# Stick-breaking attention: the weighted sums of two spans in one run of TensorE, every second step

## The chip, the cores and the metric

The kernel runs on one core of a Trainium2 chip. The metric is the device time of one execution in microseconds (us), from the profile of that core or from timed runs without a profile.

## What is computed

One step of a two-layer decoder: a retention layer, a projection to shared keys and values, and a layer of stick-breaking attention over them. The change lies in the attention of that last layer, for a prompt of 1024 tokens, 16 heads of width 64, and for eight sample sequences of 8 new tokens over 256 cached ones:

```python
z = jnp.einsum('bqhd,bkhd->bhqk', qi, k).astype(F32) * scale + bias_f
mask = (k_pos[None, :] < pi[:, None])[None, None]
log_keep = jnp.where(mask, jax.nn.log_sigmoid(-z), 0.0)
tail = lax.cumsum(log_keep, axis=3, reverse=True)
tail_excl = jnp.concatenate([tail[..., 1:], jnp.zeros_like(tail[..., :1])], axis=-1)
w = jnp.where(mask, jnp.exp(jax.nn.log_sigmoid(z) + tail_excl), 0.0)
return jnp.einsum('bhqk,bkhd->bqhd', w, v)
```

The kernel takes the products of the keeps, sigmoid(-z), instead of sums of their logarithms: `keep` is sigmoid(-z), `take` is sigmoid(z), and a weight is `take` times the running product of the keeps of all later keys.

## The kernel before

The attention is cut into pieces (`pieces`, lines 1389 to 1403). Heads go in eight pairs; a pair has eight blocks of 128 queries (a unit, 64 in all); a unit is taken in one or two spans of at most 512 keys; a span of over 256 keys makes two pieces, one for each head, and a narrower one makes one piece with both heads. A piece "closes" when the weights of both heads of its span exist: the piece of head 1, or the only one. With the eight sample pieces in the second half there are 168 pieces, numbered from 0; 96 of the prompt's pieces close.

Every engine walks through the pieces in program order, one step for each piece. At step p:

- TensorE (PE) runs `score(p + 1)` (L1768, L1769: two products for each head into one of two banks `z`), then in some steps `turn_pages` (L1744, cached keys of a sample), then `turn_w(p - 3)` (L1778: 128x128 transposes of the finished weights into one of two banks `wt`), then `attend(p - 4)`, which does nothing for a piece that does not close, and for one that does multiplies the turned weights of both heads with the values (L1806: matmuls of 64 columns, two side by side in the array, 2 for each 128 keys). In between, in the first half, `project` puts slices of three matmuls (L2959 to L2961) of the projection of the gates, in three places of a step. `fold` and `attend_sample` (L1836, L1827) belong to the samples.
- ScalarE (ACT) runs `stick(p)` (L1917: `keep`, then `take`), then `take_w(p - 3)` (L1928: copies the turned weights from `wt` to the ring `w_t`) for two pieces of three, and opens gates now and then (L1962).
- VectorE (DVE) runs `scan(p - 1)` (L2029), `take_w(p - 3)` (L2038) for every third piece, and `gate` (L2085), the product of a finished block of sums with the gates.
- GpSimd (POOL) runs `weigh(p)` (L1705), `take` times the scanned products.

Two waits tie PE to ACT. `score(p + 1)` waits until `stick(p - 1)` has emptied its bank `z`. ACT reaches `stick(p - 1)` only after `take_w(p - 5)`, the copy of a piece that PE turned in step p - 2. `attend(p - 4)` waits for the copy of piece p - 4, and it does so for pieces that do not close too:

```python
            def attend(p):
                at = pieces[p]
                wait_taken(pe, p)
```

The ring `w_t` has WR = 4 slots: a copy of piece p waits until the sums that read piece p - 4 are done. The gates' projection ends at step 65 (`G_END`); after it SP loads the inputs of the samples (`load_samples`), and at step 71 PE turns the first of them (`turn_new`, L1731). SP loads the values of a pair (`load_v`) 4 steps after the pair before it has ended. A row of biases is loaded to `bias_row` (L2624) and copied by DVE to `bias` (L2822), long before the attention starts. After the last piece PE goes on with the first products of the output layer (L1889).

Of the kernel before, what the change touches and what calls it, by code (L numbers as in the profile page):

```python
# [23 lines left out]
P = 128  # L24
# [3 lines left out]
NPT = SEQ // P  # L28
# [9 lines left out]
AH = 16  # L38
# [1263 lines left out]
class PairBuffers:  # L1302


    def __init__(self, nc):
        self.at = at = -(-nc.sbuf_base // 32) * 32

        def sb(name, shape, dt=F32):
            nonlocal at
            made = nc.alloc_sbuf_tensor_at(f"pa_{name}", shape, dt, offset=at)  # L1310
            at += -(-4 * math.prod(shape[1:]) // 32) * 32
            return made

        self.parts = nc.alloc_sbuf_tensor_at("kq_parts_q", [P, 2, 2, NB // P, P], F32R, offset=at)
        self.k_t = sb("k_t0", [P, 2, SEQ], F32R)
        self.q_hi = sb("q_hi0", [P, 2, SEQ], F32R)
        self.gates_at = at
        self.g_t = sb("g_t", [P, 2, SEQ])
        self.head_rows = sb("head_rows", [AH, P])
        self.bias_row = sb("bias_row", [P, AH])  # L1320
        self.bias = sb("bias", [P, 2, AH])
        self.queries_at = at
        self.q_lo = sb("q_lo0", [P, 2, SEQ], F32R)
        self.g_out = sb("g_out", [P, 2, NB])
        self.end = at
# [48 lines left out]
def attention(nc, t_in, t_out, ps, proj, first, sa, held, pairs, kq_stored, ctx, sem):  # L1374


    with ctx:
# [67 lines left out]

        LAG, TR, WR, KR = 3, 5, 4, 3
        sb("pairs", [P, (pairs.end - pairs.at) // 4])
# [121 lines left out]
        def wait_taken(engine, p):  # L1569
# [3 lines left out]
            else:  # L1573
                engine.wait_ge(w_taken_a, len([n for n in range(p + 1) if not on_vector(n)]))

        def sample_before(p, lag):

            return pieces[p - lag].b if p >= lag else None
# [9 lines left out]
        def _(sp):  # L1588
# [50 lines left out]
            load_g(1)  # L1639
            v_slots = {ends[NPT * pair - 1] + 4: pair + 1 for pair in range(1, PAIRS - 1)}  # L1640
            g_slots = {ends[NPT * pair - 1] + 8: pair + 1 for pair in range(1, PAIRS - 1)}
# [81 lines left out]
        def _(pe):  # L1723
# [59 lines left out]
# [3 lines that stand above are left out]
                if at.b is not None:  # L1786
                    attend_sample(p, at.b)
                    return
                if not at.closes:
                    return  # L1790
                if len(at.heads) == 1:
# [68 lines left out]
            for p in range(NPC):  # L1860
# [9 lines left out]
                project(slices_before(p, 1), slices_before(p, 2))  # L1870
                if p >= LAG + 1:
                    attend(p - LAG - 1)
                project(slices_before(p, 2), slices_before(p + 1, 0))
                if p == G_END + 2:
                    turn_gates()
                if sample_before(p, LAG + 3) is not None:
                    fold(sample_before(p, LAG + 3))
            for p in range(NPC, NPC + LAG):
                turn_w(p - LAG)
                attend(p - LAG - 1)  # L1880
            attend(NPC - 1)
            pe.wait_ge(next_loaded, 16)
# [114 lines left out]
        def _(dve):  # L1997
# [91 lines left out]

            def gate_at(p):  # L2090
                if pieces[p].u is not None and p == ends[pieces[p].u] and pieces[p].u % 4 == 3:
                    gate(pieces[p].u)

# [21 lines left out]
            for p in range(NPC):  # L2115
                if p:
                    scan(p - 1)
                if p >= LAG:
                    take_w(p - LAG)
                if p >= LAG + 2:  # L2120
                    gate_at(p - LAG - 2)
                for t in steps_done_at(p):
# [10 lines left out]
            for p in range(NPC - LAG, NPC):  # L2133
                take_w(p)
            for p in range(NPC - LAG - 2, NPC):
                gate_at(p)
# [312 lines left out]
def shared_kv_and_queries(nc, t_in, t_out, ps, x, rated, proj, pairs, kq_stored, handed, block, sem):  # L2449
# [6 lines left out]
    with ctx:  # L2456
# [132 lines left out]
        def _(sp):  # L2589
# [32 lines left out]
            for n in range(2):  # L2622
                sp.wait_ge(parts_stored[n], 16 * NPT // 2)
            sp.dma_start(pairs.bias_row[:], t_in["sb_bias"].to_broadcast([P, AH])).then_inc(consts, 16)  # L2624
            for n in range(2):
# [121 lines left out]
        def _(dve):  # L2747
# [7 lines left out]
            for s, (c, t) in enumerate(steps):  # L2755
# [64 lines left out]
                if c == GATES and t == AHEAD_AT:  # L2820
                    dve.wait_ge(consts, 16)
                    nc.vector.tensor_copy(pairs.bias[:, 0], pairs.bias_row[:])  # L2822
                    nc.vector.tensor_scalar(pairs.bias[:, 1], pairs.bias_row[:], -1.0, None, ALU.mult)

# [399 lines left out]
```

## Time and profile before

| | us |
|---|---|
| median of three timed runs | 1826.2 (1821.4 to 1829.25) |
| the profiled execution | 1827.52 |
| its span in the trace | 1825.9 |
| attention, step 1 to the last copy of weights, about | 1374 to 1715 |
| PE busy over the span | 1773.8 (97%) |
| DVE, ACT, POOL busy | 966.6, 777.1, 266.8 |

Busy time is the union of an engine's instructions. A matmul is pipelined: it is shown for longer than the engine is kept by it, and the next one starts while it is shown. What PE needs for a group of matmuls is therefore read from start to start, not from the durations.

### The profile page before, as it was taken

To read this page: it belongs to the slowest core of one execution; us is meant where nothing else is said; L and a number is where in the kernel's file an instruction comes from. 1 tells how busy PE (TensorE), PEld (TensorE's weight loads), DVE (VectorE), ACT (ScalarE), POOL (GpSimd) and SP (SyncE) were. 2 spreads that over 40 slices of the span, in tenths; PEclk is the share of its full clock that TensorE was granted. 3 is DMA by queue.
4 is the path that set the end of the run, shared out by engine and by line. 5 is a ranking of instruction groups with operands and counts; after the bars stand their busy time and mean duration, and the time that the engine had idled before them with its cause. 6 is when DMAs were issued, how large, how long until landed. Compare 5 with 4: busy or idle time off the path is not lost. (4 is left out here: it accounts for less than half of the span.)

```text
span 1825.9 us, 27331 instructions
## 1 busy us (share of the span) xinstructions
PE 1773.8 (97%) x9783; PEld 1394.7 (76%) x9783; DVE 966.6 (53%) x1836; ACT 777.1 (43%) x1651; POOL 266.8 (15%) x324
## 2 busy tenths in 40 slices
PE   5999999999999999999999999999999999999998
PEld 2778787878787878777787877888877777677677
DVE  4563535353535353543546455676615666877652
ACT  3842323232323232332234333353326677888620
POOL 2000000000000000000000012101114554555300
PEclk8999999999999999999999999999999998999999
DMA  9231313131313131465524578424355557795342
GB/s 335 87 96 60 96 59 95 59 95 59 95 59 95 59 95 59 159 219 153 149 75 137 186 213 271 138 85 130 122 146 129 129 128 237 194 240 179 97 158 98
DMA packets 153688, 240.59 MB, mean 132 GB/s; under 512 B 13208, under 2 KB 102096, under 8 KB 152561
## 3 DMA queue, kind: packets, MB, share of 16 engines
q1 hardware_dynamic: 136570, 179.69, 33.3%
q0 software_dynamic: 17024, 59.66, 9.2%
q8 instruction: 57, 0.93, 0.2%
q14 instruction: 37, 0.30, 0.1%
HBM read 177.91 MB, written 61.42 MB: 131 GB/s over the span
## 5 line engine op out<-in xcount | busy, mean ns | idle before, releaser
L484 PE MATMUL rt_acc<-rt_w_hi,rt_h_hi 128*128 128x512 f32 x504 | 203.3, 403 | 1.0 <-DVE rt_h_lo L1026 1.0
L486 PE MATMUL rt_acc<-rt_w_hi,rt_h_lo 128*128 128x512 f32 x504 | 197.1, 391 | 0.0
L485 PE MATMUL rt_acc<-rt_w_lo,rt_h_hi 128*128 128x512 f32 x504 | 196.5, 390 | 0.0
L1705 POOL TENSOR_TENSOR pa_take<-pa_take,pa_after_key 128x512 f32<-128x512 f32 (+2 forms) x152 | 152.9, 1009 | 140.0 <-DVE pa_after_key L2029 135.1
L1069 DVE TENSOR_TENSOR rt_by_cos<-rt_raw,rt_cos 128x256 f32<-128x256 f32 (+1 forms) x72 | 30.6, 425 | 242.9 <-ACT rt_raw L899 242.9
L910 ACT COPY rt_qk_t<-rt_tr 128x256 f32<-128x256 f32 (+1 forms) x72 | 26.1, 362 | 277.5 <-PE rt_tr L718 277.5
L2971 PE MATMUL kq_acc<-kq_w_hi,kq_h 128*128 128x512 f32 x320 | 128.6, 402 | 0.0
L2974 PE MATMUL kq_acc<-kq_w_hi,kq_h 128*128 128x512 f32 x320 | 125.1, 391 | 0.0
L2972 PE MATMUL kq_acc<-kq_w_lo,kq_h 128*128 128x512 f32 x320 | 124.8, 390 | 0.0
L1917 ACT ACTIVATE pa_keep<-z,pa_bias 128x128 f32<-128x128 f32 (+3 forms) x192 | 111.2, 601 | 2.9 <-PE z L1769 2.5
L1917 ACT ACTIVATE pa_take<-z,pa_bias 128x128 f32<-128x128 f32 (+3 forms) x192 | 111.3, 604 | 0.0
L486 PEld LDWEIGHTS rt_acc<-rt_w_hi,rt_h_lo 128*128 128x128 f32 x504 | 94.6, 188 | 20.6
L484 PEld LDWEIGHTS rt_acc<-rt_w_hi,rt_h_hi 128*128 128x128 f32 x504 | 94.9, 188 | 19.2 <-DVE rt_h_lo L1026 1.4
L485 PEld LDWEIGHTS rt_acc<-rt_w_lo,rt_h_hi 128*128 128x128 f32 x504 | 94.9, 188 | 17.9 <-issue 0.2
L776 PE MATMUL rt_acc_g<-rt_h_hi,rt_g_hi 128*128 128x512 f32 x256 | 105.6, 413 | 0.0
L2029 DVE TENSOR_TENSOR_SCAN pa_after_key<-pa_keep,pa_eye 128x384 f32<-128x384 f32 (+3 forms) x112 | 93.2, 850 | 18.0 <-POOL pa_take L1705 10.5
L777 PE MATMUL rt_acc_g<-rt_h_hi,rt_g_lo 128*128 128x512 f32 x256 | 100.1, 391 | 0.0
L778 PE MATMUL rt_acc_g<-rt_h_lo,rt_g_hi 128*128 128x512 f32 x256 | 100.1, 391 | 0.0
L1778 PE MATMUL pa_wt<-ident,pa_take 128*128 128x128 f32 x592 | 94.7, 278 | 0.8 <-POOL pa_take L1705 0.6
L1778 PEld LDWEIGHTS pa_wt<-ident,pa_take 128*128 128x128 f32 x592 | 71.7, 142 | 19.5 <-POOL pa_take L1705 4.1
L1806 PE MATMUL pa_out<-pa_w_t,pa_v 128*64 128x128 f32 x1152 | 85.3, 284 | 0.9 <-ACT pa_w_t L1928 0.3
L2029 DVE TENSOR_TENSOR_SCAN pa_after_key<-pa_keep,pa_after_key,pa_eye 128x512 f32<-128x512 f32 x64 | 81.7, 1277 | 8.2 <-ACT pa_keep L1917 5.2
(407 smaller groups left out, 4035.8 us busy)
## 6 DMA issues: line engine op xcount, KB each, us to landing
ro_a_raw<-retained SPq DMA_DIRECT2D x14, 1024.0 KB, 5.9
rt_w_raw<-in_ret_w_in SPq DMA_DIRECT2D x16, 512.0 KB, 5.2
rt_w_raw<-in_ret_w_in SPq DMA_DIRECT2D x8, 1024.0 KB, 8.0
rt_old<-in_state_ret SPq DMA_DIRECT2D x8, 1024.0 KB, 6.0
rt_g_raw<-in_ret_w_in SPq DMA_DIRECT2D x8, 1024.0 KB, 5.3
out_st_sample<-rt_new POOLq DMA_DIRECT2D x8, 1024.0 KB, 8.1
k_cols<-kq_parts POOLq DMA_DIRECT2D x16, 512.0 KB, 4.0
kq_w_raw<-in_sb_w_in SPq DMA_DIRECT2D x4, 2048.0 KB, 10.5
```

The lines of the kernel that those rows point to most:

```text
L484: nc.tensor.matmul(dst, h_hi[:, k, cols], w_hi[:, k, :], start=k == 0, stop=False)
L485: nc.tensor.matmul(dst, h_hi[:, k, cols], w_lo[:, k, :], start=False, stop=False)
L486: last = nc.tensor.matmul(dst, h_lo[:, k, cols], w_hi[:, k, :], start=False, stop=k == KD - 1)
L776: nc.tensor.matmul(dst, g_hi[:, k, part], h_hi[:, k, cols], start=k == 0, stop=False)
L777: nc.tensor.matmul(dst, g_lo[:, k, part], h_hi[:, k, cols], start=False, stop=False)
L1705: nc.gpsimd.tensor_tensor(own, own, later, ALU.mult).then_inc(weighed, 1)
L1778: last = nc.tensor.transpose(dst[:, b * P:(b + 1) * P], take(p)[:, b * P:(b + 1) * P], ps.ident[:])
L1917: last = nc.scalar.activation(dst[:, cols], z[:, p % 2, cols], ACT.Sigmoid, scale=(2 * part - 1) * DH ** -0.5, bias=shift)
L2029: nc.vector.tensor_tensor_scan(ring[:, c0:c0 + n][:, ::-1], k[:, ::-1], opening, seed, ALU.mult, join).then_inc(scanned, 1)
L2971: nc.tensor.matmul(dst, hi, w_hi, start=k == 0, stop=False)
L2972: last = nc.tensor.matmul(dst, hi, w_lo, start=False, stop=t == NPT and k == KD - 1)
L2974: last = nc.tensor.matmul(dst, proj.lo(t)[:, k, :], w_hi, start=False, stop=k == KD - 1)
```

## The change

`bias_row` goes, and the row of biases is loaded to `bias[:, 0]`, where it is used. `WR`, the number of slots of the ring of turned weights, goes from 4 to 5. `attend` is no longer called one step after `turn_w` of its piece: closing pieces are held back in twos, and both are summed one after the other four steps behind the second of them. A piece is summed alone where the unit is the last of four of a block of output, or a sample comes. Pieces that do not close are no longer waited for. The gates follow the new order, and SP takes up `load_v` one step later.

```diff
-        self.bias_row = sb("bias_row", [P, AH])
...
-        LAG, TR, WR, KR = 3, 5, 4, 3
+        LAG, TR, WR, KR = 3, 5, 5, 3
...
+        batches, held_back = {}, []
+        for p, at in enumerate(pieces):
+            if at.b is not None and held_back:
+                batches[held_back[-1] + LAG + 1] = held_back
+                held_back = []
+            if at.closes:
+                held_back = held_back + [p]
+            if at.b is not None or len(held_back) == 2 or at.closes and at.last and at.u % 4 == 3:
+                batches[p + LAG + 1] = held_back
+                held_back = []
+        attend_step = {p: step for step, batch in batches.items() for p in batch}
+        gate_step = {attend_step[ends[u]] + 1: u for u in range(3, UNITS, 4)}
...
-            v_slots = {ends[NPT * pair - 1] + 4: pair + 1 for pair in range(1, PAIRS - 1)}
+            v_slots = {ends[NPT * pair - 1] + 5: pair + 1 for pair in range(1, PAIRS - 1)}
...
-                if not at.closes:
-                    return
...
-                if p >= LAG + 1:
-                    attend(p - LAG - 1)
+                for q in batches.get(p, ()):
+                    attend(q)
...
-            for p in range(NPC, NPC + LAG):
-                turn_w(p - LAG)
-                attend(p - LAG - 1)
-            attend(NPC - 1)
+            for p in range(NPC, NPC + LAG + 1):
+                if p < NPC + LAG:
+                    turn_w(p - LAG)
+                for q in batches.get(p, ()):
+                    attend(q)
...
-            def gate_at(p):
-                if pieces[p].u is not None and p == ends[pieces[p].u] and pieces[p].u % 4 == 3:
-                    gate(pieces[p].u)
+            def gate_at(step):
+                if step in gate_step:
+                    gate(gate_step[step])
...
-                if p >= LAG + 2:
-                    gate_at(p - LAG - 2)
+                gate_at(p)
...
-            sp.dma_start(pairs.bias_row[:], t_in["sb_bias"].to_broadcast([P, AH])).then_inc(consts, 16)
+            sp.dma_start(pairs.bias[:, 0], t_in["sb_bias"].to_broadcast([P, AH])).then_inc(consts, 16)
...
-                    nc.vector.tensor_copy(pairs.bias[:, 0], pairs.bias_row[:])
-                    nc.vector.tensor_scalar(pairs.bias[:, 1], pairs.bias_row[:], -1.0, None, ALU.mult)
+                    nc.vector.tensor_scalar(pairs.bias[:, 1], pairs.bias[:, 0], -1.0, None, ALU.mult)
```

What moves on PE is seen at two places. The first is in the first half, steps 17 to 19, with slices of the projection. Before (L1768 and L1769 are `score`, L1778 `turn_w`, L2959 to L2961 `project`, L1806 the sums; x6 are the sums of piece 13, x8 those of piece 15):

```order
L1778 MATMUL pa_wt<-ident,pa_take 128x128 x4
L1806 MATMUL pa_out<-pa_w_t,pa_v 64x128 x6
L1768 MATMUL z<-pa_k_t_3429,pa_q_hi_3430 128x512
L1769 MATMUL z<-pa_k_t_3429,pa_q_lo_3435 128x512
L1778 MATMUL pa_wt<-ident,pa_take 128x128 x4
L1768 MATMUL z<-pa_k_t,pa_q_hi 128x512
L1769 MATMUL z<-pa_k_t,pa_q_lo 128x512
L1778 MATMUL pa_wt<-ident,pa_take 128x128 x4
L1806 MATMUL pa_out<-pa_w_t,pa_v 64x128 x8
```

The same place in the changed kernel (L1781, L1782 are now `score`, L1791 `turn_w`, L1817 the sums):

```order
L1791 MATMUL pa_wt<-ident,pa_take 128x128 x4
L1781 MATMUL z<-pa_k_t_3429,pa_q_hi_3430 128x512
L1782 MATMUL z<-pa_k_t_3429,pa_q_lo_3434 128x512
L1791 MATMUL pa_wt<-ident,pa_take 128x128 x4
L1781 MATMUL z<-pa_k_t,pa_q_hi 128x512
L1782 MATMUL z<-pa_k_t,pa_q_lo 128x512
L1791 MATMUL pa_wt<-ident,pa_take 128x128 x4
L1817 MATMUL pa_out<-pa_w_t,pa_v 64x128 x14
```

The six matmuls of piece 13 have moved past two scores and two turns, to stand with the eight of piece 15. The second place is in the second half, steps 156 to 158, without a projection. Before (L1836 is a sample's `fold`, L1757 the score of a sample; x6 are the sums of piece 152, x8 those of piece 154):

```order
L1768 MATMUL z<-pa_k_t,pa_q_hi 128x512
L1769 MATMUL z<-pa_k_t,pa_q_lo 128x512
L1778 MATMUL pa_wt<-ident,pa_take 128x128 x4
L1806 MATMUL pa_out<-pa_w_t,pa_v 64x128 x6
L1836 MATMUL pa_acc<-sa_by_group,sa_o_own 128x32 x2
L1768 MATMUL z<-pa_k_t,pa_q_hi 128x128
L1769 MATMUL z<-pa_k_t,pa_q_lo 128x128
L1768 MATMUL z<-pa_k_t,pa_q_hi 128x128
L1769 MATMUL z<-pa_k_t,pa_q_lo 128x128
L1778 MATMUL pa_wt<-ident,pa_take 128x128 x4
L1757 MATMUL z<-sa_k_t,sa_q_diag 32x320 x8
L1778 MATMUL pa_wt<-ident,pa_take 128x128 x4
L1806 MATMUL pa_out<-pa_w_t,pa_v 64x128 x8
```

And now:

```order
L1781 MATMUL z<-pa_k_t,pa_q_hi 128x512
L1782 MATMUL z<-pa_k_t,pa_q_lo 128x512
L1791 MATMUL pa_wt<-ident,pa_take 128x128 x4
L1847 MATMUL pa_acc<-sa_by_group,sa_o_own 128x32 x2
L1781 MATMUL z<-pa_k_t,pa_q_hi 128x128
L1782 MATMUL z<-pa_k_t,pa_q_lo 128x128
L1781 MATMUL z<-pa_k_t,pa_q_hi 128x128
L1782 MATMUL z<-pa_k_t,pa_q_lo 128x128
L1791 MATMUL pa_wt<-ident,pa_take 128x128 x4
L1770 MATMUL z<-sa_k_t,sa_q_diag 32x320 x8
L1791 MATMUL pa_wt<-ident,pa_take 128x128 x4
L1817 MATMUL pa_out<-pa_w_t,pa_v 64x128 x14
```

Here too the sums of the earlier piece have moved past two scores and two turns. In the whole program the groups of such matmuls fall from 95 (two of the 96 pieces already stood together, at the end) to 53.

## Rows read from the trace of the kernel before

**Rows 1.** Busy time in stretches (start:end, length, engines, PEclk, DMA share, GB/s)
```profile
1374.00:1510.00 136.00, 133.06 (x984) 103.58 (x983) 90.99 (x110) 99.07 (x198) 68.61 (x73) 0.99 0.54 127
1576.00:1712.00 136.00, 134.20 (x1310) 97.30 (x1310) 104.24 (x142) 117.61 (x252) 72.80 (x76) 1.00 0.67 187
```

**Rows 2.** Waits of 1374 to 1712 us: who for whom, us, times, longest
```profile
PEld z L1768 <- ACT pa_take L1917: 6.8, 22, 1.7
PEld pa_wt L1778 <- POOL pa_take L1705: 4.1, 8, 0.7
PEld pa_out L1806 <- ACT pa_w_t L1928: 4.0, 15, 0.6
...
PEld pa_out L1806 <- DVE pa_w_t L2038: 2.0, 7, 0.5
```

**Rows 3.** PE in order of time, turn and score without sums between: start, shown, what
```profile
1684.40 0.50 PE L1768 MATMUL z<-pa_k_t,pa_q_hi 128*128 128x512 f32 x1
...
1684.97 0.60 PE L1778 MATMUL pa_wt<-ident,pa_take 128*128 128x128 f32 x4
1685.32 0.48 PE L1768 MATMUL z<-pa_k_t,pa_q_hi 128*128 128x512 f32 x1
1685.64 0.40 PE L1769 MATMUL z<-pa_k_t,pa_q_lo 128*128 128x512 f32 x1
```

**Rows 4.** PE in order of time, sums between turn and score
```profile
1697.98 0.60 PE L1778 MATMUL pa_wt<-ident,pa_take 128*128 128x128 f32 x4
1698.51 0.66 PE L1806 MATMUL pa_out<-pa_w_t,pa_v 128*64 128x128 f32 x8
1699.10 0.50 PE L1768 MATMUL z<-pa_k_t,pa_q_hi 128*128 128x512 f32 x1
1699.44 0.40 PE L1769 MATMUL z<-pa_k_t,pa_q_lo 128*128 128x512 f32 x1
```

**Rows 5.** PE in order of time, steps 17 to 19
```profile
1410.37 0.88 PE L1806 MATMUL pa_out<-pa_w_t,pa_v 128*64 128x128 f32 x12
...
1412.82 0.47 PE L1768 MATMUL z<-pa_k_t,pa_q_hi 128*128 128x512 f32 x1 [0.47 <-issue]
```

**Rows 6.** ACT in order of time, steps 17 and 18
```profile
1410.47 0.59 ACT L1928 COPY pa_w_t<-pa_wt 128x512 f32<-128x512 f32 x1 [0.64 <-PE pa_wt L1778]
1410.95 0.60 ACT L1962 ACTIVATE pa_g_out<-pa_acc 128x512 f32<-128x512 f32 x1
1411.44 0.70 ACT L1917 ACTIVATE pa_keep<-z,pa_bias 128x512 f32<-128x512 f32 x1
1412.02 0.70 ACT L1917 ACTIVATE pa_take<-z,pa_bias 128x512 f32<-128x512 f32 x1
```

**Rows 7.** PE in order of time, steps 156 to 158
```profile
1692.29 0.88 PE L1806 MATMUL pa_out<-pa_w_t,pa_v 128*64 128x128 f32 x12
...
1693.56 0.30 PE L1768 MATMUL z<-pa_k_t,pa_q_hi 128*128 128x128 f32 x1
...
1694.60 1.28 PE L1757 MATMUL z<-sa_k_t,sa_q_diag 128*32 128x320 f32 x16
```

**Rows 8.** ACT in order of time, the takes of pieces 156 and 157
```profile
1692.45 0.69 ACT L1917 ACTIVATE pa_take<-z,pa_bias 128x512 f32<-128x512 f32 x1
...
1693.60 0.71 ACT L1917 ACTIVATE pa_take<-z,pa_bias 128x512 f32<-128x512 f32 x1
```

**Rows 9.** ACT in order of time, the take of piece 29
```profile
1435.73 0.69 ACT L1917 ACTIVATE pa_take<-z,pa_bias 128x512 f32<-128x512 f32 x1
```

**Rows 10.** PE in order of time, the score of piece 31
```profile
1437.80 0.33 PE L1768 MATMUL z<-pa_k_t,pa_q_hi 128*128 128x128 f32 x1
```

**Rows 11.** PE in order of time: the samples' gate
```profile
1525.58 1.11 PE L1731 MATMUL pa_wt<-ident,sa_new_rows 64*128 64x64 f32 x8 [2.18 <-DMA sa_by_group<-in_by_group]
```

**Rows 12.** Busy time of the stretch behind that wait
```profile
1525.00:1535.00 10.00, 9.42 (x52) 6.59 (x52) 2.17 (x4) 4.59 (x8) 2.60 (x4) 0.50 1.02 410
```

**Rows 13.** DVE in order of time: the copy of the biases
```profile
1326.33 0.18 DVE L2822 COPY pa_bias<-pa_bias_row 128x16 f32<-128x16 f32 x1 [0.45 <-DMA pa_bias_row<-in_sb_bias]
```

More of the change, by code:

```diff
@@ L1574, in wait_taken @@
                 engine.wait_ge(w_taken_a, len([n for n in range(p + 1) if not on_vector(n)]))
+        batches, held_back = {}, []
[10 more added lines that the diff above has]
+        gate_step = {attend_step[ends[u]] + 1: u for u in range(3, UNITS, 4)}
+        assert len(attend_step) == sums_done(NPC - 1) and len(gate_step) == UNITS // 4
         def sample_before(p, lag):
@@ L2134, in _ @@
                 take_w(p)
-            for p in range(NPC - LAG - 2, NPC):
+            for p in range(NPC, NPC + LAG + 3):
                 gate_at(p)
```

## The prediction

> **What bounds the kernel now.** I read the stretches of busy time first: in the attention PE is busy 133.1 of 136 us in the first half (1374 to 1510 us) and 134.2 of 136 us in most of the second (1576 to 1712 us), ACT 99.1 and 117.6 us [rows 1]. So PE sets the pace, but ACT has only 13% to spare in the second half against 27% in the first. Busy time does not tell a stall that is shorter than the tail of the last matmul, so I then read the waits: PE waits 6.8 us for `take` before a score, 4.1 us for POOL before a turn, and 4.0 and 2.0 us for copies before the sums [rows 2]. Last I read both engines in order of time, from start to start, at the places where the change moves sums.
>
> **What one merge saves.** Turn, score with no sums between: from the turn's first start to the start of L1769 is 1685.64 - 1684.97 = 0.67 us [rows 3]. With the sums of a 256-wide piece between it is 1699.44 - 1697.98 = 1.46 us [rows 4], 0.79 more. Eight records stand there, in pairs side by side, 0.11 us a pair (x12 is shown for 0.88 us and x8 for 0.66: two pairs in 0.22 us) [rows 4, 5]. Four pairs are 0.44 us, so going over to these half-width matmuls and back costs 0.35 us beside them. Groups fall from 95 to 53. Of the 43 batches of two, the last was together already: 42 x 0.35 = 14.7 us of PE's work goes at most.
>
> **What it moves.** The first piece's sums leave the place in front of two scores. Those scores wait for ACT to have emptied the bank. Call the margin the time from the end of that take to the score. Moving a 384-wide piece's sums takes 6 x 0.11 + 0.35 = 1.01 us out in front of the scores and puts 0.66 us back two steps later.
>
> Where the margin is wide, 0.35 us is gained. For the batch of pieces 25 and 27 the take of piece 29 ends at 1435.73 + 0.69 = 1436.42 us [rows 9] and score 31 starts at 1437.80 [rows 10]: 1.38 us, more than 1.01.
>
> Where it is narrow, PE gets to the score early and waits. For pieces 13 and 15: ACT's copy follows the turn of piece 14, it opens gates, and its take ends at 1412.02 + 0.70 = 1412.72 us [rows 6]; the score starts at 1412.82, the earliest it can, after an idle 0.47 us [rows 5]. Taking 1.01 us out in front gains nothing, and 0.66 us come back: a loss of about 0.6 us. For pieces 152 and 154: takes end at 1693.14 and 1694.31 us [rows 8], scores start at 1693.56 and 1694.60 [rows 7]. Less the 0.07 us from a take's end to a score, 0.22 us can be gained against 0.66 put back: a loss of 0.44 us.
>
> I made this comparison for all batches, each with the starts and ends of its own steps:
>
> - up to step 59: 17 batches; 11 have the margin (3.9 us gained), 6 lose 2.7 us together: 1.2 us gained;
> - steps 60 to 71: 3 batches. They lie in front of the samples' gate, where PE waits 2.18 us for a DMA [rows 11]. What comes before shortens the way to it, and the wait grows by the same: 0, between 1 us gained and 1 us lost;
> - steps 72 to 96: 8 batches, 2 with margin (0.7), 6 lose 0.8: 0.1 us lost;
> - steps 97 to 134: 7 batches, none with margin: 3.4 us lost;
> - steps 135 to 161: 6 batches, none with the full margin: 2.2 us lost.
>
> That is 4.5 us lost, if every take stays where it is. The last two batches stand in the tail. The one of 166 and 167 changes nothing; the sums of 163, now run while POOL works on the last pieces, move behind two turns: about 0.7 us lost, between 0 and 1.2 (its own eight pairs and 0.35).
>
> **What is given back.** First, the waits of the sums for their copies, 4.0 + 2.0 us [rows 2]. The first piece of a batch has long been copied, and its sums give the second one's copy about a microsecond more; pieces that do not close are no longer waited for. Single batches keep theirs. I take 4 us, between 0 (they come back in front of the score) and 6. Second, the takes do not stay where they are: ACT idles 0.64 us before a copy until PE has turned [rows 6], so an earlier turn brings an earlier copy and an earlier take. The bounds are 0 and the whole way from 4.5 us lost to 38 x 0.35 = 13.3 us gained, 17.8 us. I take 3 us, a sixth of it, since a step without sums takes PE 1685.32 - 1684.40 = 0.92 us [rows 3], and ACT for such a piece twice 1412.02 - 1411.44 = 0.58 us and, in two steps of three, 1410.95 - 1410.47 = 0.48 us for a copy [rows 6], 1.5 us. Three short steps in a row are now run at ACT's pace, and the double sums in the fourth leave ACT idle, since it can be ahead by no more than the two banks.
>
> **Small edits, at nothing.** DVE's copy of the biases, 0.18 us, lies 40 us before the attention, beside PE's products [rows 13]: between 0 and 0.2 us gained. The row now lands in its place, with the same issue on SP. The values of a pair are asked for one step (2 us) later on SP's queue, some 20 steps before use; what is queued behind them are the gates of the next pair, as far from use. Their cover is that distance; gone, it would show as a wait of PE for a DMA, of which there is one now, the samples'. The fifth slot keeps copies from waiting: a copy of p needs the sums of p - 5, which stand ahead of its turn in PE's order. With four it would have been a new wait.
>
> **The sum.** 4.5 + 0.7 - 4 - 3 = 1.8 us gained on 1827.5 us, which gives 1825.7. The profiled execution stands 1.3 us above the median. I predict **1826 us**: no change that can be told, a measurement here telling about 0.5% (9.1 us).
>
> **The rivals.**
> 1. *PE's work alone counts* (0.23). For it: PE is 98% busy. Against it: margins of 0.03 to 0.4 us in front of most scores of the second half. If ACT followed PE everywhere, 13.3 + 4 us would go: 1810 us. It decides faster when less than about half of the 17.8 us is lost.
> 2. *The chain behind ACT comes late as well* (0.10). Place: the turns after a double sum. ACT idles during it, so DVE's scans (over 1 us for a wide piece) and POOL's product start late, and the turns of the short steps wait for POOL. It waits so 8 times now for 4.1 us [rows 2], 0.5 us each. If the 25 batches with narrow margins each add such a wait, and nothing is given back by ACT's earlier takes: 1827.5 + 4.5 + 0.7 + 12.5 - 4 = 1841 us. It ends slower from 17 such waits on. Against it: from a score to the turn of the same piece there are always four steps, of which one is now the long one, so the time for the chain is the same over four.
> 3. *The clock falls in the new waits* (0.05). After the wait of 2.18 us PE ran at a granted clock of 0.50, that is 1.2 GHz, over 1525 to 1535 us [rows 11, 12]. Ten microseconds so cost up to 5. Waits for ACT of up to 1.7 us [rows 2] lie in stretches granted 0.99 to 1.00 [rows 1], and by the margins the new ones are about 1 us. One fall gives 1831, two 1836. The Trainium skill ("TensorE: Matmul & The Clock Gate", on HAM oscillation) says that idle gaps between bursts of matmuls bring the half clock back, which speaks against a change that puts PE's work into bursts; the trace agrees for the gate and shows no fall at the short waits.
> 4. That the merging does not happen is excluded by the order of the instructions.
>
> **How the numbers follow.** The forecast's mechanism has 0.62, with 1817 to 1834 us as its own range (half or double what ACT takes). Same: 0.58 of it, 0.02 of the first rival, 0.02 of the third, 0.62 in all. Faster by over 0.5%: 0.21 of the first rival, 0.02 of the forecast, 0.23. Slower: 0.10 of the second, 0.03 of the third, 0.02 of the forecast, 0.15. The range is 1811 to 1837: it leaves out the lower half of the first rival and most of the second.
>
> **What would show it.** Right: 53 groups of sums, 0.35 us beside each; in the second half PE's waits for `take` before scores grow from 7 to about 15 us, in short steps; the waits of sums for copies nearly go; the first half is a little shorter, the second a little longer. Wrong: PE's waits for `take` stay under 10 us and all stretches shrink by 0.35 us a batch (first rival), waits for POOL over 12 us (second), a granted clock under 0.9 outside the gate (third).

## The result, and the profile after

| | before | after |
|---|---|---|
| median of 16 runs each, us | 1826.16 (1821.4 to 1829.25) | 1829.11 (1824.97 to 1831.95) |
| profiled execution / its span, us | 1827.52 / 1825.9 | 1830.59 / 1829.0 |
| PE busy, us | 1773.8 | 1764.5 |

After over before is 1.0017, 95% interval 1.0009 to 1.0025: 3 us slower, beyond what the interval leaves open, where 1.8 us faster was forecast.

The stretches of busy time, the same two as in [rows 1] (columns as there). PE now has 5.9 us less busy time in the second one (128.34 against 134.20), in the same 136 us:

```profile
1374.00:1510.00 136.00, 130.29 (x999) 106.95 (x998) 93.47 (x112) 98.90 (x199) 69.70 (x74) 0.99 0.56 133
1576.00:1712.00 136.00, 128.34 (x1266) 93.59 (x1268) 99.37 (x135) 112.35 (x239) 70.83 (x73) 1.00 0.67 187
```

The waits of 1374 to 1712 us (us, times, longest), against [rows 2]:

```profile
PEld z L1781 <- ACT pa_take L1929: 24.9, 41, 2.1
...
PE z L1781 <- ACT pa_take L1929: 15.2, 24, 1.9
...
PEld pa_wt L1791 <- POOL pa_take L1718: 8.2, 10, 1.8
...
PEld pa_out L1817 <- ACT pa_w_t L1940: 1.2, 5, 0.4
```

The sums hardly wait for ACT's copies any more (4.0 us before, 1.2 now), and no wait for VectorE's copies is left (2.0 before). The wait for `take` before a score has grown from 6.8 to 24.9 us (weight loads), and that of the matmul itself, 3.7 us before, is 15.2. A weight load and the matmul behind it wait at the same place, so the two figures are not to be added.

From score to score the time moved like this (all from the lists in order of time; "forecast" is the part of the prediction by margins, without what was to be given back):

| from score to score | before | after | change | forecast by margins |
|---|---|---|---|---|
| 5 to 60 | 119.78 | 116.59 | -3.2 | -1.2 |
| 60 to 71 | 21.94 | 22.97 | +1.0 | 0, -1 to +1 |
| 72 to 97 (samples' gate in it) | 53.41 | 52.51 | -0.9 | +0.1 |
| 97 to 135 | 73.56 | 76.80 | +3.2 | +3.4 |
| 135 to 162 | 50.36 | 52.28 | +1.9 | +2.2 |

The short stretches left out are 0.1 us shorter together, and the tail, from the last score to the first product of the output layer, is 0.7 us longer. That is 2.7 us lost in the attention. Ahead of the first score the profiled execution of the changed kernel is 1.2 us longer, and behind the attention 0.9 us shorter.

The stretch from 72 to 97 cannot be read to a microsecond. In it before had a granted clock of 0.50 over 10 us [rows 12], the changed kernel for about 7 us in all (worked out from its rows of 1520 to 1540 us, shown with the rivals below). That is worth up to 1.7 us to the changed kernel, an estimate. And the kernel in which nothing is merged, below, took 1.0 us more than before from 75 to 97.

How a narrow place looks now: PE and ACT in order of time, with the scores of pieces 156, 157 and 158 (start, shown length, and in brackets the idle time before):

```profile
1693.60 0.50 PE L1781 MATMUL z<-pa_k_t,pa_q_hi 128*128 128x512 f32 x1
1693.93 0.39 PE L1782 MATMUL z<-pa_k_t,pa_q_lo 128*128 128x512 f32 x1
1694.16 0.49 PE L1791 MATMUL pa_wt<-ident,pa_take 128*128 128x128 f32 x3
1694.41 0.48 PE L1781 MATMUL z<-pa_k_t,pa_q_hi 128*128 128x512 f32 x1
...
1694.95 0.60 PE L1791 MATMUL pa_wt<-ident,pa_take 128*128 128x128 f32 x4
1695.39 0.53 PE L1847 MATMUL pa_acc<-sa_by_group,sa_o_own 128*128 128x32 f32 x4
1696.39 0.33 PE L1781 MATMUL z<-pa_k_t,pa_q_hi 128*128 128x128 f32 x1 [0.47 <-ACT pa_take L1929]
```
```profile
1694.69 0.48 ACT L1940 COPY pa_w_t<-pa_wt 128x384 f32<-128x384 f32 x1 [0.60 <-PE pa_wt L1791]
1695.06 0.69 ACT L1929 ACTIVATE pa_keep<-z,pa_bias 128x512 f32<-128x512 f32 x1
1695.65 0.69 ACT L1929 ACTIVATE pa_take<-z,pa_bias 128x512 f32<-128x512 f32 x1
```

ACT idles 0.60 us until PE turns at 1694.16, copies, takes `keep` and `take` to 1695.65 + 0.69 = 1696.34, and the score of piece 158 starts 0.05 us later. Call this **the path**: turn, ACT's copy, keep, take, score, here 1696.39 - 1694.16 = 2.23 us. PE's own work in this time is the score, a turn and a fold.

### The profile page after: what moved, and what is told of

It reads as the page before. It is cut to its first block and busy times, and to the rows that moved or that the text cites. A ratio compares the mean times of both kernels' runs of the same rounds, so it can differ in the third digit from the quotient of the medians.

```text
span 1829.0 us, 27283 instructions
## 1 busy us (share of the span) xinstructions
PE 1764.5 (96%) x9783; PEld 1396.4 (76%) x9783; DVE 966.4 (53%) x1835; ACT 774.4 (42%) x1651; POOL 266.7 (15%) x324
## 5 line engine op out<-in xcount | busy, mean ns | idle before, releaser
L1718 POOL TENSOR_TENSOR pa_take<-pa_take,pa_after_key 128x512 f32<-128x512 f32 (+2 forms) x152 | 153.1, 1010 | 140.7 <-DVE pa_after_key L2041 131.3
L1791 PE MATMUL pa_wt<-ident,pa_take 128*128 128x128 f32 x592 | 94.4, 277 | 5.5 <-POOL pa_take L1718 3.5
L1781 PE MATMUL z<-pa_k_t,pa_q_hi 128*128 128x128 f32 (+3 forms) x192 | 76.0, 404 | 18.7 <-ACT pa_take L1929 15.2
L1791 PEld LDWEIGHTS pa_wt<-ident,pa_take 128*128 128x128 f32 x592 | 71.0, 142 | 25.6 <-POOL pa_take L1718 9.3
L2041 DVE TENSOR_TENSOR_SCAN pa_after_key<-pa_keep,pa_after_key,pa_eye 128x512 f32<-128x512 f32 x64 | 81.7, 1277 | 11.1 <-ACT pa_keep L1929 8.1
```

The source lines that it names most:

```text
L1718: nc.gpsimd.tensor_tensor(own, own, later, ALU.mult).then_inc(weighed, 1)
L1791: last = nc.tensor.transpose(dst[:, b * P:(b + 1) * P], take(p)[:, b * P:(b + 1) * P], ps.ident[:])
L2041: nc.vector.tensor_tensor_scan(ring[:, c0:c0 + n][:, ::-1], k[:, ::-1], opening, seed, ALU.mult, join).then_inc(scanned, 1)
```

## The experiments

Thirteen kernels ran. Each ratio is to the kernel before, from runs on the same chip. Of the 43 batches of two, 13 are *wide* (the margin in the trace of before held the moved sums) and 25 *narrow*. The three ahead of the samples' gate and the two in the tail are in neither list.

### Which merges gain

The order of the sums was put under a table, all else as in the changed kernel:

```diff
-        batches, held_back = {}, []
+        MERGED = ()
+        held_back = {a: b for a, b in MERGED}
+        batches = {}
         for p, at in enumerate(pieces):
...
+            if (at.closes or at.b is not None) and p not in held_back:
+                batches[p + LAG + 1] = [a for a, b in MERGED if b == p] + [p]
```

In the next two runs MERGED holds the pairs of one kind, and the other pieces are summed singly.

**None merged** (five slots, the bias row and the later `load_v` kept).

> Everything of the change but the merging: five slots, the biases loaded in place, the load of values one step later, no wait for pieces that do not close; every closing piece is summed alone, four steps behind it. My theory (the merging alone makes the difference, by PE's wait for ACT's takes before a score): within 1 us of the kernel before, PE's waits for take before L1768's counterpart near 7 us as before. Rival (one of the other edits costs, or earns and hides a larger loss of the merging): over 2 us away from the kernel before.

Measured: 1825.4 us, ratio 0.9998 (0.9989 to 1.0007). All edits but the merging are worth nothing that can be told. The expectation was wrong in one thing: the weight loads' wait for `take` is not near 7 us but 12.0, and that for POOL 7.3 (4.1 before). So 5 us of the growth from 6.8 to 24.9, and most of that from 4.1 to 8.2 for POOL, come without any merging and cost no time.

**Only the wide ones.**

> Merges only the 13 batches whose margin between ACT's take and the next score was found wide enough before (11 up to step 59, pieces 68 and 70, pieces 89 and 91). Margin theory: each gains its whole 0.35 us, 4.5 us less than the kernel before, about 1821.6 us (ratio 0.9975). Rival (a merge costs alike wherever it stands, 43 of them 3 us): 0.9 us more, ratio 1.0005.

Measured: 1821.84 us, ratio 0.9981 (0.9969 to 0.9993). 13 x 0.35 = 4.6 us were expected, about 3.5 came, and the wait for `take` stayed at 11.7 us (12.0 with none merged).

**Only the narrow ones.**

> Merges only the 25 batches whose margin was found too narrow. Margin theory: what the changed kernel loses comes from these; it is 3 us slower than before with the 4.5 us of the wide ones gained, so these alone make it 5 to 9 us slower, about 1833 us (ratio 1.003 to 1.005), and PE's waits for take grow from 7 to over 20 us. Rival (a merge costs alike everywhere): 1.7 us more, ratio 1.001.

Measured: 1831.35 us, ratio 1.0035 (1.0022 to 1.0048), 6 us lost, with 24.0 us of waits for `take`:

```profile
PEld z L1777 <- ACT pa_take L1925: 24.0, 44, 1.7
...
PE z L1777 <- ACT pa_take L1925: 13.4, 23, 1.4
```

The stretches of this run from score 97 on lose 3.3 and 1.9 us, those of the changed kernel 3.2 and 1.9. By the ratios the two kinds alone are worth -3.5 and +6.4 us, together 2.9 us slower, about the 3.1 of the whole change. By their margins alone the narrow ones were to lose 9.1 us (2.7 + 0.8 + 3.4 + 2.2).

### The fifth slot

```diff
-        LAG, TR, WR, KR = 3, 5, 5, 3
+        LAG, TR, WR, KR = 3, 5, 4, 3
```

> The changed kernel with the ring of turned weights back at four slots. A copy of piece p now waits for the sums of piece p - 4, which in a batch of two 512-wide spans are run after the turn of p. My theory: the copy, and the next take behind it on ACT, comes about 2 us later after each double sum of four single-head pieces; some 20 such batches, a part of it hidden: 5 to 20 us slower than the changed kernel. Rival (the slot is not needed, since the copies lag anyway): within 2 us of the changed kernel.

Measured: 1830.47 us, ratio 1.0029 (1.0018 to 1.0040), some 2 us over the changed kernel, with intervals that overlap. This expectation, and the prediction's "with four it would have been a new wait", were wrong in size: the fifth slot is hardly used.

### A third bank for the scores

PSUM is full, so a third bank `z` needs the bank in which a constant of the scans, `eye`, lies. It went to SBUF.

```diff
-        z, wt, acc, eye, out = held.z, bank("wt", 2), bank("acc"), bank("eye"), bank("out", 2)
+        z, wt, acc, z_own, eye, out = held.z, bank("wt", 2), bank("acc"), bank("z2"), ps.eye, bank("out", 2)
...
-                if p >= 2:
-                    pe.wait_ge(sticks, p - 1)
+                if p >= 3:
+                    pe.wait_ge(sticks, p - 2)
```

First the control, two banks, `eye` in SBUF, none merged:

> Control for the next two: every closing piece summed alone as in the kernel before, five slots, and the constant that the scans open with moved from a bank of PSUM to SBUF, so that a bank is free but unused. All theories: within 1.5 us of the kernel before; the scans' mean changes by under 5%.

Measured: 1849.38 us, ratio 1.0132 (1.0114 to 1.0149). So the control is no neutral one: the scans became slower. Groups of instructions, scans of DVE (busy, mean ns of one), of the changed kernel and of the control:

```profile
L2041 DVE TENSOR_TENSOR_SCAN pa_after_key<-pa_keep,pa_after_key,pa_eye 128x512 f32<-128x512 f32 x64 | 81.7, 1277 | 11.1 <-ACT pa_keep L1929 8.1
```
```profile
L2045 DVE TENSOR_TENSOR_SCAN pa_after_key<-pa_keep,pa_after_key,pa_eye 128x512 f32<-128x512 f32 x64 | 119.4, 1866 | 4.1 <-issue 0.5
```

Three banks, none merged:

> As the control, but the freed bank is a third bank for scores: a score waits for the take before the last, not for the last. No merging. Margin theory: PE's waits for take before a score (12 us in the run without merging) mostly go; 4 to 8 us less than the control, unless they come back as waits for POOL or for copies. Rival (ACT's total work is the bound of the second half, not the depth of its queue): under 1.5 us less.

Measured: 1851.81 us, 1.0138 (1.0118 to 1.0158). Three banks, all merged:

> Three banks for scores and all 43 batches merged. Margin theory: the merging's loss came from scores waiting for the bank, so with one more bank the merging gains most of its 0.35 us a batch: 8 to 13 us less than the kernel with three banks and no merging, and well below both kernels, about 1810 us; waits for take under 8 us. Rival (ACT idles through a double sum whatever the banks, since it has one scored piece ahead only, and is the bound over four steps): within 3 us of the kernel with three banks and no merging.

Measured: 1850.83 us, 1.0138 (1.0119 to 1.0158). The weight loads' waits for `take` fell from 11.9 us in the control to 2.3 and 1.5 us, but with all merged they waited 37.6 us for POOL before turns. VectorE was busy for 329 of the 371 us from 1374 to 1745, in the changed kernel for 254. The pair is inconclusive: it shows that the third bank removes the wait for `take`, not what that would be worth with fast scans. That wasn't tried.

### ACT's work, or the path

**Every second copy on VectorE** instead of every third, all merged: ACT has about 13 us less to do.

```diff
-            return at.b is None and p % 3 == 0
+            return at.b is None and p % 2 == 0
```

> The changed kernel with every second copy of turned weights on DVE instead of every third, so ACT has one copy of about 0.49 us less in six steps, some 28 copies or 13 us of work less. If ACT's work in the short steps is what PE waits for, PE's waits for take fall from 25 to under 18 us and the time by 3 to 8 us against the changed kernel. Rival (the chain of scans on DVE and products on POOL is as near to its limit): waits for POOL before turns grow from 9 us by as much, and the time stays or rises.

Measured: 1829.53 us, ratio 1.0024 (1.0014 to 1.0033); waits for `take` 25.7 us, as without this edit. The rival's mark did not come either: the waits for POOL fell, from 8.2 to 1.8 us. The stretches say more. Score 5 to 60 took 113.85 us, 2.7 less than in the changed kernel: there it helps that ACT has one copy less in the path. 60 to 71 and 97 to 135 took 27.16 and 78.98, 4.2 and 2.2 more. In each of the two stands a longer wait of PE, and in or behind it the granted clock falls. The first, with the clock of 1511 to 1517 us and the double sum in it, which took 1.97 us in the changed kernel (last line):

```profile
1511.06 0.58 PE L1781 MATMUL z<-pa_k_t,pa_q_hi 128*128 128x256 f32 x1 [2.94 <-ACT pa_take L1929]
...
1512.85 3.68 PE L1817 MATMUL pa_out<-pa_w_t,pa_v 128*64 128x128 f32 x32
```
```profile
1511.00:1517.00 6.00, 5.94 (x43) 5.24 (x43) 3.59 (x4) 3.08 (x8) 3.56 (x4) 0.50 1.05 246
```
```profile
1515.28 1.97 PE L1817 MATMUL pa_out<-pa_w_t,pa_v 128*64 128x128 f32 x32
```

The changed kernel waits 1.91 us at this place. ACT comes late to this take because two operations of VectorE's for a sample now stand behind a copy: it idles 2.33 us for them, where it idled 0.42. So of the 4.2 us about 1 is the longer wait, and up to 3 are the clock (6 us at half of it). In the second stretch PE waits 1.79 us for a copy of VectorE's before a turn at 1629.74, and behind it, at a granted clock of 0.66 over 1629 to 1634 us, a double sum takes 3.12 us where one of the same length, shown further below, takes 1.75. How much of either loss would come in an execution without these falls, one profile does not tell.

**ACT's copy one step later**, behind the next piece's `keep` and `take`. This takes turn and copy out of the path.

```diff
+                if p >= LAG + 1:
+                    take_w(p - LAG - 1)
                 if p in new_slots and new_slots[p] < 2:
...
-                if p >= LAG:
-                    take_w(p - LAG)
...
-            for p in range(NPC - LAG, NPC):
+            for p in range(NPC - LAG - 1, NPC):
```

All merged:

> The changed kernel with one thing moved: ACT copies the turned weights of piece p - 4, not p - 3, in step p, ahead of its gates, still behind keep and take (VectorE's copies stay). So the takes of step p no longer stand behind the copy of a piece that PE has turned in that same step. Theory 'path' (after a double sum a score waits along turn, ACT's copy, keep and take, about 2.2 us, however little ACT has to do): the path is cut, PE's waits for take before scores (24.9 + 15.2 us in the changed kernel) fall by half or more, and the time falls by 4 to 12 us against the changed kernel, to 1817 to 1825 us. Theory 'ACT's work' (three short steps run at the sum of ACT's work): waits and time stay within 3 us. Rival 'the sums wait instead': the sums' waits for copies, 1.2 us for ACT's, grow over 8 us and the time stays or gets longer.

Measured: 1828.69 us, ratio 1.0021 (1.0012 to 1.0030). The waits, 1374 to 1712 us:

```profile
PEld pa_wt L1791 <- POOL pa_take L1718: 15.9, 18, 1.8
...
PEld z L1781 <- ACT pa_take L1929: 12.6, 22, 2.2
...
PE z L1781 <- ACT pa_take L1929: 6.8, 11, 2.0
...
PE pa_wt L1791 <- ACT pa_w_t L1940: 4.7, 5, 1.1
PEld pa_out L1817 <- ACT pa_w_t L1940: 4.5, 11, 0.7
```

The path is cut: waits for `take` halved (24.9 and 15.2 to 12.6 and 6.8). The time did not follow as a whole, but its stretches did different things. Score 5 to 60 took 113.14 us, 6.6 less than before (3.2 less without the later copy). Score 60 to 71 lost 2.0 us: PE waits 1.97 us for `take` at 1508.72, and behind it the granted clock is 0.50 from 1509.4 to 1512.7. From 75 to 97 it took 5.5 us more than before, where the changed kernel took 2.9 more, the kernel with only the wide merges 2.8 and the one with none 1.0. From 97 on it lost 2.8 and 2.2 us, as much as the changed kernel (3.2 and 1.9), and the tail 1.4 us, from score 162 on. The waits that grew are those for POOL (8.2 to 15.9 us), for a copy to empty the bank `wt`, and of the sums for copies.

None merged:

> The same later copy, with no sums merged (all else as in the changed kernel). It tells what the later copy is worth by itself: with single sums no long step lies in front of three short ones. Theory 'path': the waits for take were 12 us here with the copy in its old place; they fall too, but by less, and the time is 1820 to 1825 us (1825.4 with the old place), so that merging on top of the later copy now gains at least 3 us, where on top of the old one it lost 3.7. Theory 'ACT's work': as before within 3 us, and merging still loses. If sums of a single piece now wait for the copy (4.2 us for ACT's before), they do so up to 96 times, and the time can rise by 5 to 20 us.

Measured: 1837.68 us, ratio 1.0066 (1.0050 to 1.0082). Single sums wait for the later copy (13.5 us of weight loads, 8.0 of matmuls), as the last sentence of the expectation allowed for. With the later copy merging is worth 8 to 9 us (by the ratios and by the medians); with the early one it costs 3 to 4. In the first half this run is the control for the path: score 5 to 60 took 118.54 us with the later copy and nothing merged, 113.14 with all merged, so the merges gain 5.4 us there. With the early copy it is 119.38 against 116.59, 2.8 us.

**Both, later copy and every second copy on VectorE.**

> All merges, ACT's copy one step later, and in addition every second copy given to VectorE instead of every third. In the two runs that had one of these each, the time did not move: PE's waits for take fell from 40 to 19 us with the later copy, but those for POOL grew from 12 to 20 and those for copies from 2 to 13. Theory 'ACT's work stands behind the path': with the path cut, about 13 us less work of ACT now counts; waits for take and copies together fall under 20 us, and the time is 1820 us or less. Theory 'the chain keep, scan, weigh, turn stands behind it': waits for POOL grow to 25 us or more, since VectorE has more to copy, and the time stays within 3 us of 1828.7 or gets longer.

Measured: 1829.99 us, ratio 1.0027 (1.0016 to 1.0039). Neither theory fits: waits for `take` are back at 16.6 us, those for POOL 10.0. Score 5 to 60 took 113.73 us, 97 to 135 took 77.95, 135 to 162 took 50.83, the last 1.4 less than in the changed kernel.

### The price of a group by itself

```diff
+                for q in batches.get(p, ())[:-1]:
+                    attend(q)
                 if p >= LAG:
                     turn_w(p - LAG)
                 project(slices_before(p, 1), slices_before(p, 2))
-                for q in batches.get(p, ()):
+                for q in batches.get(p, ())[-1:]:
                     attend(q)
```

> The changed kernel with the same batches in the same steps, but the first piece's sums run in front of the turn and the second piece's behind it, so that they no longer stand side by side: 95 groups of sums as before the change, in the order of work of the changed kernel. It measures the 0.35 us of a group by itself. If PE sets the pace in these steps, 42 x 0.35 = 14.7 us are added: 1844 us. If the step is followed by waits for ACT that take it up, less: the sum of waits for take (40 us) lies largely in the steps behind, but the path that they wait on starts behind the double sum, so I expect at least 10 us more, 1839 us. If it adds under 4 us, a group's price was hidden or not 0.35 us.

Measured: 1836.98 us, ratio 1.0071 (1.0054 to 1.0088), against 1.0017: 0.0054 x 1826 = 9.9 us for 42 groups more, just under the 10 expected, and 0.24 us for each (the two intervals leave some 3 us either way). One place of each in order of time, first split, then side by side in the changed kernel:

```profile
1414.92 0.40 PE L1782 MATMUL z<-pa_k_t,pa_q_lo 128*128 128x512 f32 x1
1415.24 0.88 PE L1817 MATMUL pa_out<-pa_w_t,pa_v 128*64 128x128 f32 x12
1416.05 0.66 PE L1791 MATMUL pa_wt<-ident,pa_take 128*128 128x128 f32 x4
1416.64 1.09 PE L1817 MATMUL pa_out<-pa_w_t,pa_v 128*64 128x128 f32 x16
```
```profile
1413.17 0.50 PE L1781 MATMUL z<-pa_k_t,pa_q_hi 128*128 128x512 f32 x1 [1.42 <-ACT pa_take L1929]
1413.51 0.40 PE L1782 MATMUL z<-pa_k_t,pa_q_lo 128*128 128x512 f32 x1
1413.74 0.60 PE L1791 MATMUL pa_wt<-ident,pa_take 128*128 128x128 f32 x4
1414.27 1.75 PE L1817 MATMUL pa_out<-pa_w_t,pa_v 128*64 128x128 f32 x28
```

From the start of L1782 to that of the last sums: 1.72 us in the first. In the second 0.76 us to the first pair, and six pairs (6 x 0.11 = 0.66) more to the same point, 1.42: the group costs 0.30 us here. The price is real: of 42 x 0.35 = 14.7 us two thirds were paid, in a kernel that waits in many places.

### Put together

Up to step 60 the later copy and all 17 merges, from there on the early copy and the two wide merges only:

```diff
+        LATE = 60
...
+                if LAG < p <= LATE:
+                    take_w(p - LAG - 1)
                 if p in new_slots and new_slots[p] < 2:
...
-                if p >= LAG:
+                if p >= LATE:
                     take_w(p - LAG)
```

> A version put together from the stretches of the earlier runs. Up to step 60: all 17 merges, with ACT's copy one step later (in the run with the later copy throughout, score 5 to score 60 took 113.14 us, before 119.78: 6.6 gained, which is 17 x 0.35 and a little more). From step 60 on: ACT's copy in its old place, and only the two merges with a wide margin there (68 with 70, 89 with 91), since all others lost. Theory 'margin and path, by stretch': 6.6 + 0.7 = 7.3 us less than before: 1818.5 us, ratio 0.996, faster than both kernels and than the version with the 13 wide merges (0.9981). Rival 'stretches do not add' (the gain of the first half is taken back in front of the samples' gate, by the wait for the DMA there): 1824 us or more, ratio 0.999 to 1.0.

Measured: 1816.2 us, ratio 0.9955 (0.9940 to 0.9970): 8 us faster than before and, by the two ratios, 11 faster than the changed kernel. Score 5 to 60 took 113.00 us; 97 to 135 and 135 to 162 took 73.28 and 50.31, as before the change. The waits for `take` are those of the kernel without merges:

```profile
PEld z L1778 <- ACT pa_take L1926: 12.0, 29, 1.7
...
PEld pa_wt L1788 <- POOL pa_take L1715: 7.8, 12, 1.8
```

Behind the samples' gate this run has a granted clock of 1.00 where before had 0.50 [rows 12], and score 72 to 97 took 4.7 us less than before, of which the one merge there should account for 0.35. From the first score to the first product of the output layer the profiled execution is 10.8 us shorter than that of before. So 6 us lie outside that stretch, against the 7.3 expected, and most of the 4.7 is the clock of the two executions compared (10 us at half of it cost up to 5). The ratio is over timed runs, in which the clock differs too: at the same mean clock, 0.989, four runs of before took 1826.7 us on the mean and one of this kernel 1819.6. The gain is clear of noise, and without the clock's part it is better put at 6 to 7 us than at 8.

## Why the prediction was wrong

By its own steps:

- **What one merge saves**, 0.35 us: right or a little high. Split groups cost 9.9 us for 42, 0.24 each, in a kernel that waits in part, and 0.30 us at the place measured. There are 53 groups, as said.
- **What it moves**: right in the second half. By margins 3.4 and 2.2 us were to be lost from score 97 on, 3.2 and 1.9 were. The tail lost 0.7 us as forecast. The wide and the narrow merges, run apart, came out on the two sides that their margins gave. In the first half 3.2 us were gained for 1.2 by margins.
- **What is given back**, 4 + 3 us: this is the step that failed. By margins and tail 5.2 us were to be lost, 2.7 were (3.0 by the medians): some 2.5 us were given back, not 7, and by the clock around the gate it may be less. Of these, 2.0 us came in the first half and 0.5 from score 97 on. The waits of the sums for copies did nearly go (4.0 to 1.2 us for ACT's), but the time did not follow, while the waits in front of the score doubled (12.0 us with nothing merged, 24.9); that the ones became the others is likely and not shown place by place. And the takes came earlier by less than said. The text let an earlier turn bring an earlier take, and took for the limit ACT's work in three short steps. In sizing this it left out the path: 2.23 us from a turn to the score two places on, which a shorter step of PE does not shorten. For the first half this is shown: with ACT's copy out of the path, the same merges gain 5.4 us instead of 2.8, each against its own kernel without merges. For the second half it is shown only that the path is where PE waits, not that it is the one limit: there the cut path brought other waits and no time.
- **The small edits**, at nothing: right (ratio 0.9998). That the fifth slot spares a new wait: wrong in size, about 2 us at most.
- **The sum**: 1.8 us gained; 2.7 lost. The 4.5 us between are the term above. The 1826 us stand on the profiled execution of 1827.5 us; taken from the median, 1826.2, the same sum would have been 1824.4.
- **The rivals.** PE's work alone did not count. The chain behind ACT came late only where the later copy had made room for it (waits for POOL 15.9 us); in the changed kernel they rose from 4.1 to 8.2, under the 12 us set as a mark, and were at 7.3 with nothing merged. The third was set aside too lightly. That the trace shows no fall at the short waits is a reading of a mean over 136 us, which hides short ones: before, behind a wait of 1.34 us for ACT stands a stretch of 4 us with a granted clock of 0.57.

```profile
1376.63 0.45 PE L1768 MATMUL z<-pa_k_t,pa_q_hi 128*128 128x384 f32 x1 [1.34 <-ACT pa_take L1917]
```
```profile
1378.00:1382.00 4.00, 4.00 (x15) 3.25 (x14) 2.66 (x4) 1.95 (x4) 2.79 (x4) 0.57 1.04 212
```

The changed kernel has a fall at the same place too, while the kernels with only the narrow merges, with four slots and with half the copies on VectorE have the same wait, 1.33 us, and none. The changed kernel has none behind its new waits in the two long stretches (1.4 us at the longest) nor behind that of 1.91 us at 1514.28. With four slots, with the later copy, with half the copies on VectorE and with both, the clock did fall in or behind the wait at that place (1.91, 1.97, 2.94 and 3.00 us); with the groups split it did not, at 1.91 us. So merging lengthens a wait (0.85 us before) at which the clock can fall, and whether it does differs from one profiled execution to another; that the wait is its cause is not shown by an experiment. Around the gate it was otherwise than before, 0.81 to 0.84 over 20 us where before had 1.00, 0.50 [rows 12] and 0.97; the granted clock stands third from the right:

```profile
1520.00:1525.00 5.00, 4.16 (x26) 3.03 (x28) 3.45 (x5) 4.03 (x10) 4.98 (x5) 0.81 1.04 402
1525.00:1535.00 10.00, 8.30 (x70) 6.44 (x68) 5.62 (x11) 6.82 (x13) 2.85 (x4) 0.84 0.90 357
1535.00:1540.00 5.00, 5.00 (x40) 4.24 (x36) 2.71 (x4) 2.55 (x6) 1.31 (x2) 0.83 0.00 0
```

- **What would show it**: waits for `take` were to grow to about 15 us; they grew to 24.9, from 12.0 by the merging. That mark told of the error.

What stays open is what would have to move for the merges of the second half to gain. Each of the three reliefs tried with all merges (fewer copies on ACT, later copies, both) left the time within 2 us of the changed kernel, by the ratios: waits for POOL, for copies and for the bank `wt` took over, and no run tells one of them apart as the bound.

## What to carry to other kernels

An engine that is 97% busy can still be one whose work, made shorter, gives nothing: compare at each place the time that the move takes out in front of a wait with the margin behind the releaser's end, and price what comes back later at full. Don't count on the releaser coming earlier unless the whole path that leads to it has been followed; where a copy of the turned data stands in it, move the copy behind the work that the wait is for (here it paid in the first half only). And choose by place: 13 merges with margin gained 3.5 us together, 25 without lost 6.4. Read the clock stretch by stretch before a difference between two profiled executions is put down to an edit: a mean over a long stretch does not show a fall of a few microseconds.

## What was not expected of the hardware

With `eye` in SBUF the scans took 1866 ns instead of 1277 for 512 keys. The longer ones overlap GpSimd's products: of the 96 scans of 512 keys in the control, the 10 that run beside no product take 1.24 us on the mean, the 43 that run beside one for 0.9 to 1.1 us take 2.14. In the changed kernel it is 1.25 and 1.26 us, beside a product or not. DVE and POOL of the control in order of time:

```profile
1599.70 1.75 DVE L2045 TENSOR_TENSOR_SCAN pa_after_key<-pa_keep,pa_eye 128x512 f32<-128x512 f32 x1
...
1607.02 1.28 DVE L2045 TENSOR_TENSOR_SCAN pa_after_key<-pa_keep,pa_after_key,pa_eye 128x512 f32<-128x512 f32 x1 [0.25 <-DVE pa_g_t L2101]
```
```profile
1599.27 1.09 POOL L1722 TENSOR_TENSOR pa_take<-pa_take,pa_after_key 128x512 f32<-128x512 f32 x1 [1.16 <-DVE pa_after_key L2045]
...
1605.67 1.09 POOL L1722 TENSOR_TENSOR pa_take<-pa_take,pa_after_key 128x512 f32<-128x512 f32 x1 [1.16 <-DVE pa_after_key L2045]
1608.39 1.09 POOL L1722 TENSOR_TENSOR pa_take<-pa_take,pa_after_key 128x512 f32<-128x512 f32 x1 [1.62 <-ACT pa_take L1933]
```

The scan at 1599.70 overlaps a product that ends at 1600.36 and takes 1.75 us; the one at 1607.02 runs between two products, which end at 1606.76 and start at 1608.39, and takes 1.28 us, its old time. POOL's products kept their length (1010 and 1011 ns on the mean). So it is a price of running beside POOL with both inputs in SBUF, and VectorE pays it alone. The Trainium skill ("VectorE: DVE Perf Modes", section "Two Vector instructions with no wait between them") says in passing that an instruction's second tensor in SBUF is read through an interface that is shared with GpSimd; the trace agrees, and gives the price, about 0.6 us for a scan of 512 on the mean here and 0.9 where a whole product runs beside it.
